# Keys and queries of 1024 tokens of an mLSTM layer in seven block products, on one NeuronCore

## What is computed

```python
p = h @ w_in                      # q, k, v, o, g of 8 heads x 128, and gates
qc, kc, vc = ...                  # chunks of 128 tokens, kc scaled by DK ** -0.5
s = einsum('blhd,bshd->bhls', qc, kc) * w
num = einsum('bhls,bshe->blhe', s, vc) + w0t * einsum('blhd,bhde->blhe', qc, C)
C_new = decay * C + einsum('bshd,bshe->bhde', kw, vc)     # kw = kc * wk
n_new = decay * n + sum(kw)
hm = (hf + flip(hb)) * sigmoid(o)                          # forward and backward scan
y = (hm * silu(g)) @ w_out
```

## Time and profile before

| | |
|---|---|
| median of 3 runs | 2601.29 us (2600.39 to 2602.07) |
| the profiled execution | 2602.68 us |
| its span | 2600.9 us, 49722 instructions |
| PE busy | 2553.8 us, 98% |
| DVE, ACT, POOL busy | 1271.7, 928.8, 659.3 us |
| heads | about 1228 to 2410 us |

### The profile page before, as it was taken

How to read it: one execution, slowest core, us unless ns; L and a number is a source line. 1 busy time by engine, 2 the same in 40 slices (tenths; PEclk the granted TensorE clock), 3 DMA queues, 4 the chain that set the end, 5 groups by cost and what they waited for, 6 DMA issues and landing times.

```text
span 2600.9 us, 49722 instructions
## 1 busy us (share of the span) xinstructions
PE 2553.8 (98%) x18511; PEld 2238.1 (86%) x18511; DVE 1271.7 (49%) x3329; ACT 928.8 (36%) x2157; POOL 659.3 (25%) x826
## 2 busy tenths in 40 slices
PE   6999999999999999999999999999999999999998
PEld 4788888888888887888999999999999999999776
DVE  6774645646465566553242333414233342525876
ACT  5463635626353463223122221313122131313333
POOL 1412222141222213331031120404022040403363
PEclk9999999999999999999999999999999999999999
DMA  9702112030221215432041221303132130415653
GB/s 360 263 21 71 54 55 72 18 99 11 70 59 51 71 51 183 137 125 66 23 79 45 47 85 23 101 17 88 37 62 69 34 91 17 88 44 151 221 155 128
DMA packets 190862, 223.84 MB, mean 86 GB/s; under 512 B 27328, under 2 KB 133584, under 8 KB 188704
## 3 DMA queue, kind: packets, MB, share of 16 engines
q1 hardware_dynamic: 184016, 200.13, 27.1%
q10 hardware_dynamic: 6608, 20.55, 2.0%
HBM read 182.47 MB, written 38.17 MB: 85 GB/s over the span
## 4 chain that ended last, share of the span: by engine, by line
PE 87%; DVE 4%; DMA 3%; POOL 2%; issue 2%; SPq 1%; ACT 0%; DVEq 0%; POOLq 0%; ACTq 0%
PE psum L590 18%; PE psum L592 17%; PE psum L591 17%; PE psum L1336 6%; PE psum L1316 4%; PE psum L1296 2%; PE psum L2928 2%; PE psum L1299 2%; PE psum L1651 2%; PE psum L1653 2%; PE psum L1652 2%; PE psum L2995 2%; PE psum L2998 2%; PE psum L2976 1%; DMA m_bc<-gate_rows_mlstm 1%
## 5 line engine op out<-in xcount | busy, mean ns | idle before, releaser
L590 PE MATMUL psum<-h_hi,m_w_lo 128*128 128x384 f32 (+1 forms) x1600 | 593.9, 371 | 1.3 <-DVE m_w_lo L574 1.3
L592 PE MATMUL psum<-h_hi,m_w_hi 128*128 128x384 f32 (+1 forms) x1600 | 573.5, 358 | 0.0
L591 PE MATMUL psum<-h_lo,m_w_hi 128*128 128x384 f32 (+1 forms) x1600 | 573.1, 358 | 0.0
L592 PEld LDWEIGHTS psum<-h_hi,m_w_hi 128*128 128x128 f32 x1600 | 300.5, 188 | 27.0
L590 PEld LDWEIGHTS psum<-h_hi,m_w_lo 128*128 128x128 f32 x1600 | 301.3, 188 | 26.0 <-issue 3.0
L591 PEld LDWEIGHTS psum<-h_lo,m_w_hi 128*128 128x128 f32 x1600 | 301.6, 189 | 22.3
L590 PE MATMUL psum<-h_hi,attn_w_lo 128*128 128x384 f32 (+2 forms) x816 | 297.4, 364 | 1.3 <-DVE attn_w_lo L574 1.2
L592 PE MATMUL psum<-h_hi,attn_w_hi 128*128 128x384 f32 (+2 forms) x816 | 288.9, 354 | 0.0
L591 PE MATMUL psum<-h_lo,attn_w_hi 128*128 128x384 f32 (+2 forms) x816 | 288.8, 354 | 0.0
L1078 DVE CUSTOM_DVE_ANT_0 arena<-psum,wmask,stats 128x640 f32<-128x640 f32 (+2 forms) x256 | 206.0, 839 | 75.1 <-PE psum L1299 74.5
L992 ACT ACTIVATE arena<-arena,stats 128x640 f32<-128x640 f32 (+2 forms) x272 | 213.5, 786 | 70.8 <-DVE stats L1078 69.8
(11 more groups left out here) (414 smaller groups left out, 4723.9 us busy)
## 6 DMA issues: line engine op xcount, KB each, us to landing
m_bc<-gate_rows_mlstm SPq DMA_DIRECT2D x124, 256.0 KB, 3.4
m_w_raw<-in_mlstm_w_in SPq DMA_DIRECT2D x40, 512.0 KB, 4.7
h_full<-gated_output SPq DMA_DIRECT2D x26, 512.0 KB, 4.3
gated_output<-gT SPq DMA_DIRECT2D x8, 1088.0 KB, 5.2
layer_output<-xb_out ACTq DMA_DIRECT2D x17, 512.0 KB, 2.6
h_hi_full<-layer_output SPq DMA_DIRECT2D x17, 512.0 KB, 5.8
out<-h_hi_full ACTq DMA_DIRECT2D x17, 512.0 KB, 5.4
attn_w_raw<-in_attn_w_in SPq DMA_DIRECT2D x16, 512.0 KB, 6.5
```

The lines of the kernel that those rows point to most:

```text
L590: pe.matmul(out, self.lo[:, k, :], E.h_hi[:, k, tok], start=(k == 0), stop=False)
L591: pe.matmul(out, self.hi[:, k, :], E.h_lo[:, k, tok], start=False, stop=False)
L592: ins = pe.matmul(out, self.hi[:, k, :], E.h_hi[:, k, tok], start=False, stop=(k == KT - 1))
```

## The change

For heads 1 to 7 the products of [k; q] weights with tokens 0 to 1023 are no longer made as eight blocks (two kinds, two token groups of 512, two halves of the features) but as seven (the Strassen-Winograd form), each of 12 matmuls of 512 columns. They need four sums of weight blocks S1 to S4 and four sums of token blocks T1 to T4.

The token sums are made once, ahead of and during head 0, in four rounds (one for each k-tile of a half): in each, five sums on POOL, four on DVE, four casts on POOL and four remainders on DVE; SP stores the four results (512 KB each) to DRAM, and the next round writes the same staging tiles. Round 0 stands ahead of k's cast on POOL, round 1 ahead of q's, rounds 2 and 3 behind it; on DVE round 1 stands inside the gates' chain. Each later head loads them, 16 times 512 KB, into four slots that lie in the space of the states.

Weight sums are made for each head, by POOL with the casts at the boundary of heads and by DVE; the query weights are split there too, no longer by `Projection`. Some block sums are made by DVE out of PSUM.

Head 0 keeps its ten direct units of k and q, now without key work between them. In all heads the key turns and products move into the ten units of o and g, three for each unit, with a third `kw` buffer in `bc[4]`.

On SP the g weights are loaded behind the pair; rows 0 to 3 follow; the v weights come ahead of row 4 (row 5 before), which waits for all key products; new_C and new_n are stored between rows 6 and 7 (ahead of row 0 before). At the end of a head the q weights of the next and its T2 sums are loaded ahead of the output's store. The remainder of k weights keeps its place on DVE. In `first_output` some tiles trade places, and one semaphore serves for two.

The diff, cut to its core:

```diff
+def heads_apart(eng, n, body):
+
+    body(0, True, False)
+    with eng.Fori(1, n - 1) as h:
+        body(h, False, False)
+    body(n - 1, False, True)
...
+                def store_sums(sp, k):
+                    for n, t in enumerate((T3, T2, T4, T1)):
+                        sp.wait_ge(s_slo, at(4 * k + n + 1))
+                        sp.dma_start(E.sums_dram[4 * t + k], stage[:, t, :].bitcast(F32)).then_inc(s_t[t], 16)
...
+                    def load_sum(hn, t, x):
+                        sp.dma_start(t_ring[x].bitcast(F32), E.sums_dram[4 * t + x]).then_inc(s_t[x], 16)
+
+                    def next_sum(t):
+                        for x in range(4):
+                            if x < 3:
+                                sp.wait_ge(s_tu, at(h * 12 - 12 + 3 * (t - 1) + x + 1))
+                            else:
+                                sp.wait_ge(s_pr, at(h * 7 - 7 + t + 2))
+                            settle(E, sp)
+                            load_sum(h, t, x)
...
-                    load(h * 5 + 3, "o", h)
-                    load(h * 5 + 4, "g", h)
-                    with nc.allow_non_contiguous_dma(reason="normaliser columns"):
-                        sp.wait_ge(s_kvb, at(h * NT + NT))
-                        settle(E, sp)
-                        for d in range(2):
-                            sp.dma_start(E.new_C[0, 0, d, ds(h, 1)].rearrange("a d e -> d (a e)"), cout[:, d, 0:MHD]).then_inc(s_cst, 16)
-                            sp.dma_start(E.new_n[0, 0, d, ds(h, 1)].rearrange("a d -> d a"), cout[:, d, MHD:E1]).then_inc(s_cst, 16)
+                    n_o, n_g = weights_no(h, 3), weights_no(h, 4)
+                    if first:
+                        load(n_o, "o", h)
+                        store_sums(sp, 2)
+                        store_sums(sp, 3)
+                        for t in range(4):
+                            sp.wait_ge(s_t[t], at(64))
+                    else:
+                        sp.wait_ge(s_sum, at(h * 4 + SUMS))
+                        load(n_o, "o", h)
+                        next_sum(T3)
+                        next_sum(T1)
+                        next_sum(T4)
+                        sp.wait_ge(s_pr, at(h * 7))
+                    load(n_g, "g", h)
...
+                        if c == NB - 1:
+                            if not last:
+                                load(weights_no(h, 5), "v", h + 1)
+                            sp.wait_ge(s_kv, at(h * NT + NT))
...
+                        if c == NB + 2:
+                            with nc.allow_non_contiguous_dma(reason="normaliser columns"):
+                                sp.wait_ge(s_kvb, at(h * NT + NT))
+                                settle(E, sp)
+                                for d in range(2):
+                                    sp.dma_start(E.new_C[0, 0, d, ds(h, 1)].rearrange("a d e -> d (a e)"), cout[:, d, 0:MHD]).then_inc(s_cst, 16)
+                                    sp.dma_start(E.new_n[0, 0, d, ds(h, 1)].rearrange("a d -> d a"), cout[:, d, MHD:E1]).then_inc(s_cst, 16)
                         if not last and c == NB + 3:
-                            load(h * 5 + 6, "k", h + 1)
+                            load(weights_no(h, 6), "k", h + 1)
...
+                        for free_at, x in ((12, 2), (12, 0), (14, None), (15, 3), (16, 1)):
+                            sp.wait_ge(s_num, at(h * NT + free_at))
+                            settle(E, sp)
+                            if x is None:
+                                sp.dma_start(q_raw[:, :, :], w_in[:, :, ds((h + 1) * P, P)]).then_inc(s_qraw, 16)
+                            else:
+                                load_sum(h + 1, T2, x)
...
+                def token_sums(k):
+                    for t in (T3, T2):
+                        pool.wait_ge(s_t[t], at(16 * k))
+                    settle(E, pool)
+                    pool.tensor_tensor(t_sum(T3), h_hi_of(k + 4, 1), h_hi_of(k, 1), ALU.subtract).then_inc(s_sum, 1)
+                    pool.wait_ge(s_sum, at(9 * k + 1))
+                    pool.tensor_tensor(t_sum(T3), t_sum(T3), h_lo_of(k + 4, 1), ALU.add).then_inc(s_sum, 1)
+                    pool.wait_ge(s_sum, at(9 * k + 2))
+                    pool.tensor_tensor(t_sum(T3), t_sum(T3), h_lo_of(k, 1), ALU.subtract).then_inc(s_sum, 1)
+                    pool.wait_ge(s_sum, at(9 * k + 3))
+                    pool.tensor_tensor(t_sum(T2), t_sum(T3), h_hi_of(k, 0), ALU.add).then_inc(s_sum, 1)
+                    pool.wait_ge(s_sum, at(9 * k + 4))
+                    pool.tensor_tensor(t_sum(T2), t_sum(T2), h_lo_of(k, 0), ALU.add).then_inc(s_sum, 1)
+                    pool.tensor_copy(stage[:, T3, 0:512], t_sum(T3)).then_inc(s_shi, 1)
+                    pool.wait_ge(s_sum, at(9 * k + 5))
+                    pool.tensor_copy(stage[:, T2, 0:512], t_sum(T2)).then_inc(s_shi, 1)
+                    pool.wait_ge(s_sum, at(9 * k + 7))
+                    pool.tensor_copy(stage[:, T4, 0:512], t_sum(T4)).then_inc(s_shi, 1)
+                    pool.wait_ge(s_sum, at(9 * k + 9))
+                    pool.tensor_copy(stage[:, T1, 0:512], t_sum(T1)).then_inc(s_shi, 1)
...
+                token_sums(0)
                 J.pool_hi(pool, 1, 2)
+                token_sums(1)
+                J.pool_hi(pool, 2, 3)
+                token_sums(2)
+                token_sums(3)
...
+                        pool.tensor_tensor(s1, q_raw[:, 0:4, :], q_raw[:, 4:8, :], ALU.add).then_inc(s_sum, 1)
+                        J.pool_hi(pool, n_k, n_k + 1, base, (0,))
+                        pool.wait_ge(s_num, at(h * NT))
+                        pool.wait_ge(s_sum, at(h * 4 - 3 + SUMS))
+                        settle(E, pool)
+                        pool.tensor_tensor(s2, s1, k_raw[:, 0:4, :], ALU.subtract).then_inc(s_sum, 1)
+                        J.pool_hi(pool, n_k, n_k + 1, base, (1,))
...
+                def token_sums(k):
+                    for t in (T4, T1):
+                        dve.wait_ge(s_t[t], at(16 * k))
+                    dve.wait_ge(s_sum, at(9 * k + 5))
+                    dve.tensor_tensor(t_sum(T4), h_hi_of(k + 4, 0), t_sum(T2), ALU.subtract).then_inc(s_sum, 1)
+                    dve.wait_ge(s_sum, at(9 * k + 6))
+                    dve.tensor_tensor(t_sum(T4), t_sum(T4), h_lo_of(k + 4, 0), ALU.add).then_inc(s_sum, 1)
+                    dve.tensor_tensor(t_sum(T1), h_hi_of(k + 4, 1), t_sum(T2), ALU.subtract).then_inc(s_sum, 1)
+                    dve.wait_ge(s_sum, at(9 * k + 8))
+                    dve.tensor_tensor(t_sum(T1), t_sum(T1), h_lo_of(k + 4, 1), ALU.add).then_inc(s_sum, 1)
+                    dve.wait_ge(s_sum, at(9 * k + 9))
+                    for n, t in enumerate((T3, T2, T4, T1)):
+                        dve.wait_ge(s_shi, at(4 * k + n + 1))
+                        dve.tensor_tensor(stage[:, t, 512:1024], t_sum(t), stage[:, t, 0:512], ALU.subtract).then_inc(s_slo, 1)
+                token_sums(0)
+                L.dve(dve, O.s_consts, O.s_m0, J, lambda: token_sums(1))
+                J.dve_lo(dve, 2)
+                token_sums(2)
+                token_sums(3)
...
+                    def product(out, w, k0, rest, start):
+                        hi, lo = w
+                        for k in range(4):
+                            if k0 is None:
+                                pe.wait_ge(s_t[k], at(64 * h + 16 * (rest + 1)))
+                                b_hi, b_lo = t_ring[k][:, 0:512], t_ring[k][:, 512:1024]
+                            else:
+                                b_hi, b_lo = E.h_hi[:, k0 + k, rest], E.h_lo[:, k0 + k, rest]
+                            pe.matmul(out, lo[:, k, :], b_hi, start=(start and k == 0), stop=False, skip_group_check=True)
+                            pe.matmul(out, hi[:, k, :], b_lo, start=False, stop=False, skip_group_check=True)
+                            ins = pe.matmul(out, hi[:, k, :], b_hi, start=False, stop=(k == 3), skip_group_check=True)
+                            if k0 is None and k < 3:
+                                ins.then_inc(s_tu, 1)
+                        ins.then_inc(s_pr, 1)
...
+                    def pair():
+                        early, late = slice(0, 512), slice(512, 1024)
+                        a11, a12 = ((J.hi[:, k:k + 4, :], J.lo[:, k:k + 4, :]) for k in (0, 4))
+                        a22 = (q_hi[:, 4:8, :], q_lo[:, 4:8, :])
+                        s1, s2, s3, s4 = zip(sum_hi, sum_lo)
+                        first_bank, second_bank = E.bank[0][:, :], E.bank[1][:, :]
+                        pe.wait_ge(s_P, at(h * NT))
+                        pe.wait_ge(J.s_lo, at(2 * n_k + 1))
+                        product(first_bank, a11, 0, early, True)
+                        value_turn(h, NG - 1, value_bank(NG - 1))
+                        pe.wait_ge(J.s_lo, at(2 * n_k + 2))
+                        pe.wait_ge(s_hm, at(h * NT))
+                        J.pe_slices(pe, n_k, 2, E.bank[2], 0, KT)
```

(73 more changed lines are left out.)

345 lines of the change are left out of this document (240 added, 105 removed).

## The result

The changed kernel takes 2610.6 us in the median of its runs (2609.63 to 2613.12), the kernel before 2600.4 beside it. The ratio is 1.0039, with a 95% interval of 1.0029 to 1.0049: slower by 7.5 to 12.7 us. The profiled span grew by 7.9 us, from 2600.9 to 2608.8; the profiled execution of before lay 2.3 us above its median, which is the rest of the 10.2.

The account below looks back on a forecast made before the run. It took PE, busy 1178 of 1182 us, as the bound. Terms -19.2 - 1.5 + 10 + 1.7 + 12 + 1 + 1.5 = +5.5 on 2602.68 gave 2608.2 profiled, 2607 as median; range 2588 to 2622, likeliest case 2597 to 2614.

Parts of the forecast that it names:

- Matmuls removed: Keys and queries of heads 1 to 7: seven block products of 12 matmuls for eight, 19.2 us gained.
- head boundary: Between heads: POOL's weight sums about the k cast may hold DVE's subtraction, 1.5 us lost (0 to 4).
- rival 3: Pairs of key and query units: their own waits take the 2.7 us a head gains; 2617 to 2626, chance 0.10.
- Stall removed: Head 5, ahead of the first slice of value weights: its wait and slow start go, 1.5 us gained (0 to 1.6).
- Hold of head 0: After head 0's queries: PE waits for the o weights behind token-sum rounds 2 and 3, 10 us lost (5 to 12).
- the clock: Behind head 0's wait for the o weights: PE may restart at half clock, 1.7 us lost (0 to 3.5).
- The serial end: Head 0's wait for o weights with POOL and DVE work one after the other: 11.4 us, against 5.4 side by side.
- Stores in the steps: Heads 0 to 6: row 7 lands late behind new_n's stores, 1.75 us each, 12 us lost (0 to 24).
- Head 7: Last head: the stores of new_C and new_n stand behind the output weights' loads, 1 us lost (0 to 4).
- Loads of token sums: Sixteen 512 KB loads for each head, landing before their products need them: cost nothing.
- rival 2: Block products: a load of token sums misses its product; slower, 2617 with half of it, 2628 whole; chance 0.20.
- Rival 1: Steps: row 7 comes in time despite new_n's stores; faster, about 2592 (2586 to 2596), chance 0.27.

## Why the prediction was right, and where it was not

It forecast 2607, slower by 6; the time is 2610.6, slower by 10. That the two lie this near is in part luck: head 7 cost 6 us more than its term, and the stores in the steps, the hold of head 0 and the stretch behind the heads 4.9 less. By its steps, against the profiled spans:

- **Matmuls removed, -19.2; head boundary, +1.5.** Together -17.0 measured. The products are as dense as the units they replace and wait for no load, so the 19.2 holds and 2.3 was lost about them; rival 3 falls. The run with the casts first gave 1.5 of it back (seven pairs gain 18.0 and 18.1 in the two versions that have it, 15.9 to 17.3 in the eight that don't), which shows that POOL's sums ahead of the casts were the cause of that part. 0.2 us for each pair stays unexplained.
- **Stall removed, -1.5.** -1.0: the gap is gone, 0.55 came back one step later.
- **Hold of head 0, +10 and +1.7 for the clock.** 8.0 and 1.75; 10.1 to the first scores. The working was right in its places: POOL started round 2 at 1255.84 (forecast 1255.8), so rounds 0 and 1 held nothing, and PE ran out at 1278.40 with its last matmul (1278.3). The serial end was too dear: DVE's sums beside casts took 0.97 us for 0.75 and the casts 1.0 to 1.1 for 0.62, but beside POOL's sums DVE had nothing to do, except q's remainder in round 2 (1.77 us for 0.69).
- **Stores in the steps, +12.** 10.2 for heads 0 to 6. The runs on the stores show the mechanism as stated: new_n's elements, row 7 late, PE in order. The nearness of the size is luck, since three figures were off and cancelled in part. Row 7 came after 9.0 to 10.5 us, not 8.9 to 13.2 (why the first rows of before took longer behind the same stores is not settled). Its deadline is about 8.6 us, not 9.7 (its time to POOL less the delay it caused is 8.55 to 8.59 in heads 1 to 6, 8.87 in head 0), since ACT's queue leads from row 7 to PE by a way that the prediction did not follow: it named DVE and the numerator, the wait was mostly the next head's values. And row 8, which "adds nothing" there, took 3.1 of the 10.2, row 7 7.1. The load of k weights ahead of row 8 is not the reason: with the stores ahead of row 4 and the same load ahead of it, row 8 reached POOL after 3.5 to 4.3 us for 9.4 to 10.6, and no step waited for it.
- **Head 7, +1 (0 to 4).** 7.0, 5 of it waits and 2 at a lower granted clock, for which the term had nothing: the term that was mis-sized, and outside its own bounds. The place was named (the stores stand behind the output weights' loads) and the price was a guess without a row: the 4 MB were issued 10.9 us ahead of the first scores, much as before (10.4), but before the stores were through by then, and now they come between the 4 MB and row 7. The wait for key products ahead of row 4, which the text named, is what keeps the 4 MB that late now; it did not say that they are queued behind it.
- **Loads of token sums, 0.** Right, and rival 2 fell: 112 loads landed in 5.4 us in the median, 3.7 had been the nearest row, and no product waited.

Rival 1 asked whether rows can pass the stores in the queue. They did not: with all four stores ahead, no row 7 reached POOL in under 8.97 us in heads 0 to 6 of the changed kernel. The Trainium skill ("DMA: Bandwidth & Descriptors", "Two DMAs through the same engine are not ordered") states that a later descriptor can complete while an earlier one's write is outstanding; no run here shows a row doing so past these stores. The run from ACT's queue shows that the queue is not what decides. What the packets show is that other transfers are held up beside the elements as well as behind them.

## What to carry to other kernels

When a transfer is moved in a queue, ask what it does to the DMA engines at its new place, not only what stands behind it: two stores of 128 single elements, 512 bytes each, cost nothing in the gate units, 1.5 us a head in the steps and 4 to 10 us beside a large load. For a new wait, list everything that is queued behind it for the last and the first pass of a loop too, where other transfers stand. Align two traces by the same matmul in each pass: the table of delays named every place at once, and the places that cancel.

## What was not expected of the hardware

- Beside the four stores, by the two runs that part them the two of 128 single elements (4 bytes each), the 16 DMA engines were busy at 0.6 to 1.1 in windows that moved 11 to 67 GB/s, where the 2 MB loads reach 390. The 4-byte packets took 9 ns each; a 2048-byte packet of another transfer, 0.09 us otherwise, took up to 7.8. That the stores were issued by another engine's queue made little difference (8.5 us lost in head 7 for 9.4).
- A store of 128 rows of 512 bytes between the same rows cost nothing: it landed in 2.8 to 3.1 us, and row 7 behind it in 4.3.
- DVE sums of 128x512 took 0.97 to 0.98 us where a POOL cast had started first, and 0.68 where the sum itself had (1265.00 against the cast's 1265.14); that cast then took 1.01, where one that had started first took 0.61. Casts that started behind a DVE operation took 1.01 to 1.14.
